# Stacked keys, token-major values and negated scores in the neighbourhood attention of a two-block transformer kernel

## The reference

```
h  = modulate(rms_norm_2(x, norm1), sh1, sc1);   hc = modulate(rms_norm_2(xc, norm1), csh1, csc1)
w_q, w_k, w_v = split(w_qkv)                      # 1024 x 1024 each
q = rms_norm_2(split_heads(h @ w_q), q_gain);     k, kc likewise with k_gain;   v, vc without norm
s_loc = einsum('bqhd,bqijhd->bhqij', q_row, k_win) * scale + bias      # 8 x 16 keys
s_ctx = einsum('bqhd,bkhd->bhqk', q_row, k_ctx) * scale                # 256 keys
p = softmax(concatenate([s_loc, s_ctx]))
y = (p_loc @ v_win + p_ctx @ vc) @ w_o
x = x + g1 * y                                    # then the convolutional FFN
```

## Time and profile before

| what | value |
|---|---|
| runs (3): median, lowest, highest | 1746.81, 1741.76, 1747.14 us |
| profiled execution, its span | 1741.06 us, 1739.4 us |
| mean granted clock of PE | 0.987 of full speed |
| busy: PE, DVE, ACT, POOL | 1685.8, 979.0, 757.4, 148.3 us |
| instructions: PE, DVE, ACT, POOL | 8914, 1336, 1074, 199 |
| DMA | 178.61 MB, mean 103 GB/s |

### The profile page before, as it was taken

One profiled execution on the slowest core, in us unless ns is written; L12 is line 12 of the kernel. 1 busy time (PEld: TensorE's weight loads), 2 busy tenths in 40 slices (PEclk: granted clock), 3 DMA queues, 4 the chain that ended last, 5 costly groups with the idle time before them and its releaser, 6 DMA issues.

```text
span 1739.4 us, 22656 instructions
## 1 busy us (share of the span) xinstructions
PE 1685.8 (97%) x8914; PEld 1420.7 (82%) x8914; DVE 979.0 (56%) x1336; ACT 757.4 (44%) x1074; POOL 148.3 (9%) x199
## 2 busy tenths in 40 slices
PE   6999999999999999999999999979999899999998
PEld 6888888889898788888878888867788688888887
DVE  5345554566456566556666566268884555435543
ACT  4244333334444456555553676136663333213320
POOL 3000000000000000000000000046660000000000
PEclk8999999999999999999999999979999899999999
DMA  8321222324224443565553123221102133343322
GB/s 264 91 60 49 65 81 97 122 96 145 97 97 126 116 133 117 165 200 178 174 155 114 49 73 101 99 80 40 37 10 73 54 94 89 97 113 97 89 84 81
DMA packets 227589, 178.61 MB, mean 103 GB/s; under 512 B 5971, under 2 KB 217278, under 8 KB 227502
## 3 DMA queue, kind: packets, MB, share of 16 engines
q1 hardware_dynamic: 218206, 142.74, 27.7%
q0 software_dynamic: 8576, 32.23, 5.5%
q10 hardware_dynamic: 720, 2.41, 0.4%
HBM read 171.37 MB, written 9.13 MB: 104 GB/s over the span
## 4 chain that ended last, share of the span: by engine, by line
PE 86%; DVE 5%; ACT 4%; issue 2%; POOL 2%; DMA 1%; SPq 0%; DVEq 0%; ACTq 0%; POOLq 0%
PE ps L1598 27%; PE ps L1600 26%; PE ps L1599 26%; POOL sc L2134 2%; DVE w_lo L995 1%; ACT w_hi L559 1%; PE ps L1728 1%; PE ps L2017 1%; ACT mod_tmp L682 1%; PE ps L1667 1%; ACT vt_h L928 1%; PE ps L2047 1%; DMA x_rows<-in_x 0%; PE ps L1714 0%; POOL bias L2120 0%
## 5 line engine op out<-in xcount | busy, mean ns | idle before, releaser
L1598 PE MATMUL ps<-h_hi,w_hi 128*128 128x512 f32 x1024 | 401.3, 392 | 4.7 <-DVE h_lo L1409 2.5
L1599 PE MATMUL ps<-h_lo,w_hi 128*128 128x512 f32 x1024 | 399.3, 390 | 0.0
L1600 PE MATMUL ps<-h_hi,w_lo 128*128 128x512 f32 x1024 | 399.2, 390 | 0.0
L995 DVE TENSOR_TENSOR w_lo<-w_raw,w_hi 128x2048 fp32r<-128x2048 f32 (+1 forms) x136 | 290.3, 2134 | 114.5 <-ACT w_hi L559 114.2
L559 ACT ACTIVATE w_hi<-w_raw 128x2048 fp32r<-128x2048 f32 (+1 forms) x136 | 242.4, 1782 | 151.7 <-PE ps L1600 149.0
L1598 PEld LDWEIGHTS ps<-h_hi,w_hi 128*128 128x128 f32 x1024 | 192.7, 188 | 46.0 <-DVE w_lo L995 3.2
L1600 PEld LDWEIGHTS ps<-h_hi,w_lo 128*128 128x128 f32 x1024 | 192.5, 188 | 40.7
L1599 PEld LDWEIGHTS ps<-h_lo,w_hi 128*128 128x128 f32 x1024 | 192.7, 188 | 38.5
L1598 PE MATMUL ps<-xg_hi,w_hi 128*128 128x512 f32 x352 | 139.5, 396 | 2.4 <-DVE w_lo L995 2.4
L1600 PE MATMUL ps<-xg_hi,w_lo 128*128 128x512 f32 x352 | 137.3, 390 | 0.0
L1599 PE MATMUL ps<-a_lo,w_hi 128*128 128x512 f32 x352 | 137.1, 389 | 0.0
(11 more groups left out here) (337 smaller groups left out, 3021.1 us busy)
## 6 DMA issues: line engine op xcount, KB each, us to landing
mod_raw<-in_l_w_mod POOLq DMA_DIRECT2D x24, 1024.0 KB, 7.9
w_raw<-in_w_ffn_in SPq DMA_DIRECT2D x44, 512.0 KB, 5.0
w_raw<-in_l_ffn_w_up SPq DMA_DIRECT2D x44, 512.0 KB, 5.0
w_raw<-in_w_in SPq DMA_DIRECT2D x40, 512.0 KB, 5.1
w_raw<-in_l_na_w_qkv SPq DMA_DIRECT2D x24, 512.0 KB, 4.5
w_raw<-in_w_mem_kv SPq DMA_DIRECT2D x16, 512.0 KB, 3.9
...
```

The lines of the kernel that those rows point to most:

```text
L995: v.tensor_tensor(wlo[s][:, 0:size], raw[s][:, 0:size], whi[s][:, 0:size].bitcast(F32), ALU.subtract).then_inc(w_lo, 1)
L1598: mm(o, w_h, x_h, start=first, stop=False, **kw)
L1599: mm(o, w_h, x_l, start=False, stop=False, **kw)
L1600: return mm(o, w_l, x_h, start=False, stop=last, **kw)
```

## The change

- **Keys** are stored stacked in `kst`: for a head, high parts on one half of the partitions and low parts on the other. A step's scores are two matmuls of 128 partitions and 512 columns: stationary is the query's high part, doubled on both halves, then its low part, doubled; moving are the strip's keys and the context keys together. All four products are then in the sum. k_raw has two small buffers in place of one for all heads, and `head_high` and `head_low` write each half on its own.
- **Queries**: once split, POOL spills them to q_scr (8 DMAs of 512 KB, on its queue), and SP loads each head's high and low parts to both halves of `qd` (2 DMAs of 256 KB, 64 partitions each).
- **Values** are projected token by token (`value_chunks`): 128 tokens are stationary, 256 columns of weights move; 6 blocks of tokens, 8 products of three matmuls for each, 144 matmuls a unit, context tokens first. ACT (vo_hi) and DVE (vo_lo) split them; SP spills both parts so that each strip's tokens lie together (`spill_values`, 16 DMAs of 32 partitions and 128 KB, 2 of 128 partitions and 256 KB, per unit, 2.62 MB), and loads two heads with two DMAs of 655 KB (`load_values`). vo_hi and vo_lo are single: their copies wait for the spill of the unit before (`v_spill`). Windowing, value transposes and their splits in the loop are gone.
- **Scores are negated**: the query gain carries the sign, the bias is window minus table, the custom operation takes the minimum over all 512 columns (the context's bias is zero), exp has scale -1. L1529 and L1535 are gone.
- **First scores**: S(0) and S(1), their minima, exponentials and reciprocals stand inside the last value unit.
- A head's output goes to bank 6 or 7 in turn; V(4h) waits for q_lo of the head before the last. Loops over heads are written out.

The diff, cut:

```diff
@@ SP @@
+            def load_queries(head):
+                src = q_scr[:, 64 * head:64 * head + 64, :].rearrange("l p n -> p l n")
+                for half in range(2):
+                    sp.dma_start(qd[head % 2][64 * half:64 * half + 64, :, :].bitcast(F32), src).then_inc(qd_in[head % 2], 16)
+            def spill_values(i):
+                cols = slice(256 * i, 256 * i + 256)
+                sp.wait_ge(evac, tab["na_qkv"][0] + 8 + i + 1)
+                for x, src in enumerate((vo_hi, vo_lo)):
+                    for tau in range(TT):
+                        to = v_scr[x, 256 * tau:256 * tau + 256, cols].rearrange("(q r w) f -> r w q f", q=4, r=2)
+                        for r in range(2):
+                            sp.dma_start(to[r], src[64 * r + span[tau]:64 * r + span[tau] + 32, 0:4, :].bitcast(F32)).then_inc(v_spill[i], 16)
+                    sp.dma_start(v_scr[x, 1024:1280, cols].rearrange("(q p) f -> p q f", p=P), src[:, 4:6, :].bitcast(F32)).then_inc(v_spill[i], 16)
+            qkv_unit(10)
+            spill_values(0)
+            qkv_unit(11)
+            spill_values(1)
+            na_o_unit(0)
+            sp.wait_ge(rpb_out, 16 * GRID_H)
+            sp.wait_ge(q_spill_last, 32)
+            for head in range(2):
+                load_bias(head, head)
+                load_queries(head)
+            sp.wait_ge(v_spill[0], V_SPILLED)
+            load_values(0)
+            spill_values(2)
+            na_o_unit(1)
+            spill_values(3)
+            na_o_unit(2)
+            for head in range(NA_HEADS - 2):
+                sp.wait_ge(bias_done, head + 1)
+                load_bias(head + 2, head % 2)
...
@@ ACT @@
+                if i >= 8:
+                    act.wait_ge(vc_ps, i - 7)
...
+                        act.wait_ge(v_spill[i - 9], V_SPILLED)
+                    act.activation(vo_hi[:, 4:6, :], bank(4 + s).rearrange("p (q n) -> p q n", q=2), ACT.Copy).then_inc(vo_done, 1)
+                    if i == n - 1:
+                        na_exp(0)
+                        na_exp(1)
...
@@ DVE @@
-                v.tensor_reduce(na_nmax_c[:, tau:tau + 1], ps[:, tau, 256:512], AX.X, ALU.max, negate=True)
-                v.tensor_tensor_reduce(out=ps[:, tau, 0:256], in0=ps[:, tau, 0:256],
...
-                v.scalar_tensor_tensor(na_nmax[:, tau:tau + 1], na_max[:, tau:tau + 1], -1.0, na_nmax_c[:, tau:tau + 1],
-                                       ALU.mult, ALU.min).then_inc(ns_max, 1)
+                v.tensor_tensor_reduce(out=o, in0=o, in1=bias[head % 2][:, kind:4:3 - kind, :], scale=1.0, scalar=3.0e38,
+                                       op0=ALU.add, op1=ALU.min, accum_out=na_nmax[:, tau:tau + 1]).then_inc(ns_max, 1)
@@ PE @@
+            def value_chunks(s, count, out_of, x_h, x_l, ks=range(KT)):
+                for k in ks:
+                    for q in range(count):
+                        tokens, w = slice(q * P, q * P + P), slice(256 * k, 256 * k + 256)
+                        last = product(out_of(q), x_h[:, k, tokens], x_l[:, k, tokens], whi[s][:, w], wlo[s][:, w],
+                                       k == 0 and q % 2 == 0, k == KT - 1, skip_group_check=True)
-                product(bank(tau, 256), q[0], q[1], k[0], k[1], True, True)
-                product(ps[:, tau, 256:512], q[0], q[1], c[0], c[1], True, True).then_inc(ns_ps, 1)
+                mm(o, qd[head % 2][:, 0, P * tau:P * tau + P], keys, start=True, stop=False)
+                mm(o, qd[head % 2][:, 1, P * tau:P * tau + P], keys, start=False, stop=True).then_inc(ns_ps, 1)
-                    if head:
-                        pe.wait_ge(no_lo, head)
+                    if head >= 2:
+                        pe.wait_ge(no_lo, head - 1)
+                    if i == n - 1 and k == 3:
+                        pe.wait_ge(evac, b + i)
+                        na_scores(0)
+                        na_scores(1)
```

More of the change, by code:

```diff
@@ L111, in constants @@
         key = min(max(16 * strip - 8, 0), 32) + jl
[L112 removed]
+        c[:, C_WIN + 32 * n:C_WIN + 32 * n + 32] = np.where((key >= start) & (key < start + WIN_W), 0.0, -NEG)
     return c
@@ L859, in _, with na_exp, na_out @@
             high_parts_shifted(3, 0, tb3)
+            def na_exp(g):
+                tau = g % 4
+                act.wait_ge(ns_max, g + 1)
+                if g >= 4:
+                    act.wait_ge(np_ps, g - 3)
+                act.activation(sc[:, tau, :], bank(score_bank(g)), ACT.Exp, bias=na_nmax[:, tau:tau + 1], scale=-1.0,
+                               accum_out=na_den[:, tau:tau + 1]).then_inc(ns_exp, 1)
+            def na_out(head):
+                a, half = divmod(head, 2)
+                act.wait_ge(no_ps, head + 1)
+                rows = slice(64 * half, 64 * half + 64)
+                act.activation(q_hi[rows, a, :].rearrange("p (r t c) -> p t r c", t=4, c=16),
+                               bank(6 + half)[0:64, :].rearrange("p (t r c) -> p t r c", t=4, r=8), ACT.Copy).then_inc(no_hi, 1)
             def head_squares(i, job):
@@ L961, in _ @@
+                if i == 9:
+                    act.preload_act_table(ACT.Exp)
+            for g in range(NA_G):
+                if g + 2 < NA_G:
+                    na_exp(g + 2)
+                act.wait_ge(np_ps, g + 1)
+                act.activation(np_hi[:, g % 2, :], bank(prob_bank(g)), ACT.Copy).then_inc(np_h, 1)
+                if g % 4 == 0 and g:
+                    na_out(g // 4 - 1)
+            na_out(NA_HEADS - 1)
             act.preload_act_table(ACT.Sqrt)
@@ L1551, in _ @@
-            na_pair(7, 1, last=True)
-            na_out(7, 1, NA_HEADS)
+            na_max(2)
+            for g in range(NA_G):
+                if 1 < g + 1 < NA_G:
+                    na_den_step(g + 1)
+                if g + 3 < NA_G:
+                    na_max(g + 3)
+                dve.wait_ge(np_h, g + 1)
+                low(np_lo[:, g % 2, :], bank(prob_bank(g)), np_hi[:, g % 2, :]).then_inc(np_l, 1)
+                if g % 4 == 0 and g:
+                    na_out(g // 4 - 1)
+            na_out(NA_HEADS - 1)
@@ L2135, in normalise @@
                                    ALU.mult).then_inc(ns_norm, 1)
+            pool.wait_ge(vc_ps, 4)
+            for head in range(2):
+                pool.memset(bias[head][:, 3, :], 0.0)
+                for kind in range(3):
+                    build_bias(head, kind)
             normalise(0)
-            for g in range(4 * NA_HEADS):
-                if g + 1 < 4 * NA_HEADS:
+            normalise(1)
+            for g in range(NA_G):
+                if 1 < g + 1 < NA_G:
                     normalise(g + 1)
```

419 lines of the change are left out of this document (178 added, 241 removed).

## The result

Four runs of the changed kernel have a median of 1717.29 us (1713.94 to 1718.43), four of the kernel before 1744.61 (1741.76 to 1747.14): a ratio of 0.9843, 95% interval 0.9828 to 0.9859. The profiled execution took 1718.43 us with a span of 1716.4 at a mean granted clock of 0.984; the prediction had 1716.7 for it and 1722 for the median.

The account below looks back on a forecast made before the run. The loop is nearly PE-bound, its start is not. T(3) at 1156.0 + 128.7 + 4.1 = 1288.8 against 1313.2, -24.4: profiled 1741.1 becomes 1716.7, and with the median 5.7 above, 1722; range 1708 to 1738.

Parts of the forecast that it names:

- Value units and key units: Stage na_qkv: value units +0.6 us each, +2.4 for four, scores of steps 0 and 1 add 0.9; key units 0.
- One step: Plain step of the neighbourhood loop: PE takes 1.79 us instead of 2.23, with two scores matmuls of 0.2275.
- Minimum: DVE in a loop step: one custom operation of 512 columns costs 0.34 to 0.68 us, taken as 0.65.
- Head boundary: Each head's third step: chain stays, T(4h) to T(4h+2) takes 4.92 us instead of 5.37; a head is 8.50.
- Half clock: Loop after T(3): 12.7 us at a granted clock of 0.50, 4.0 steps of 3.15 us, costing 4.1 us.
- Start of the loop: SP's queue before T(3): three spills of 8.7 us in the chain; T(3) waits for gb(2), at 1156.0.
- rival A: Strip spills and qd loads: narrow DMAs move at the low rate, T(3) about 11 us later, time 1733; chance 0.30.
- Rival B: Loop's head boundary: second out bank takes q_hi and q_lo off PE's path, 20 us less, 1702; chance 0.07.
- Rival C: Value spills: 18 small DMAs run one after another at a fixed cost; at d = 20 time 1756; chance 0.07.
- Rival D: Stacked scores: a 128-row product costs twice 0.2275, a step stays 2.24 us, time about 1740; chance 0.01.

Follow-up runs that it names:

- the wide form: Changed kernel, but each of a unit's sixteen strip spills reads 128 partitions with one 1 KB piece instead of 32 with four: 1711.67 us.

## Why the prediction was right, and where it was not

The forecast (faster, 1722, a range of 1708 to 1738) held. By its own steps:

- **Value units and key units**: from the start of the first value unit (1065.6) to the last product before the gap (1137.1) are 71.5 us; four units of 17.28, with the scores of steps 0 and 1 at 0.9 they are 70.0, and the sums and transposes for the norms, which stood there before too, are the rest. PE has no idle time in them. From the first product of the key units to the squares of the third query unit are 105.3 us before and after, so the longer work of ACT and DVE in the key units cost nothing. Right.
- **One step**: 1.69 instead of 1.79. The scores take 0.56, not 0.455; the transposes 0.41, not 0.55, and the values 0.72, not 0.78, which I had carried over from before. PE needs some 1.65 of the 1.69 by itself and POOL sets the rest; that more work of PE lengthens the step by nearly as much is shown by the doubled scores.
- **Minimum**: the operation of 512 columns takes 0.60, near the upper end as taken; the three-operation form costs 3.9 us, so DVE was close to the bound, as said.
- **Head boundary**: 2.87 and 2.75 us in turn, predicted 3.13 (4.92 less 1.79). The chain is the one described, released by POOL; moving the reciprocal ahead of q_lo took 0.73 to 0.84 of it away, and the second bank did nothing. A head is 7.88 us in the mean instead of 8.50: **15 heads give 9.2 us more than forecast**. At the end of the loop four steps and not two issue no scores, another 0.9, but T(62) waits 0.95 us for POOL there; the two nearly cancel.
- **Half clock**: the two steps after T(3) take 3.04 and 2.72 us; 2.4 above two plain ones, not 4.1. The reading of four slow steps was too many, by 1.7.
- **Start of the loop**: the failing step. T(3) was to be at 1156.0 and came at 1167.9, **11.9 us later**; 3.8 of them are the shift that lies ahead of the change, **8.1 are this step's own**. "spill(1) starts at about 1101.8" left out that unit 8's copies stand on ACT behind the last query unit's factors and high part, so that spill(0) starts only at 1091.6, and that unit 9's copies wait for it: four spills are in the chain, not three. spill(1) starts at 1109.2, with the shift taken off 3.7 late. And the spills on their own are dearer than the 8.7 us of the forecast: spill(1) takes 12.5, 3.8 more. The 300 GB/s were 252 in the first spill, where query spills and weights move beside the strips; the wide form took 4.6 us off T(3). Nor was issuing cheap: the 18 issues of spill(1) occupy SP for 8.7 us, not 5.4, and those of spill(0) 11.4. The wide form has the same 18 in 8.8 us and is faster, so issuing is not all of it; how much it is of a spill, no run tells. The mechanism behind it (third spill frees unit 11, T(3) waits for gb(2) through POOL) was right: the row of POOL says so, and with the table moved ahead T(3) went to 1155.3.

The sum: 1288.8 + 11.9 - 9.2 - 1.7 = 1289.8, measured 1290.2. That the total came out is luck in its size: the start took 8.1 us more than forecast, loop and clock 10.9 less, and a time inside the range isn't evidence that the start was read well. By its own sign, T(3) after 1163, rival A had come true; but its 11 us were 8.1 here, of which the width of the transfers explains 4.6, and its time, 1733, was off by what loop and clock gave back. Rival B's mechanism (the second bank takes the boundary off PE's path) fell. Rival C's spill time (16.8 us) was not reached by a spill on its own (12.5 to 14.8), though spill(2), with the first heads' loads ahead of it, took 17.2 from its first issue. Rival D fell.

The medians differ by 27.3 us, the profiled executions by 22.6; 3.8 of the difference between the two is the shift ahead of the change. The 5.7 us from the profiled execution to the median, which the forecast carried over, were -1.1 after: that is spread between executions and no quantity to carry.

Still open: how much of the start the query spills and loads take by themselves, how much of a spill is issuing and how much bytes, and why the transposes are followed sooner by a stacked score matmul than by a narrow one. None of these was tried.
